# Where the split tensors begin in SBUF: stationary and moving operands at multiples of 64 bytes modulo 256

## What is computed

```python
for l in range(DEPTH):                                   # DEPTH = 2
    x = x + 0.5 * swiglu(rms_norm(x, norm_ffn1[l]), ffn1_in[l], ffn1_out[l])
    h = rms_norm(x, norm_mix[l])
    proj = h @ w_in[l]                                   # 1024 x 5504
    ...                                                  # rwkv7 mixer, differential attention
    y = jnp.einsum('bsgc,gcd->bsgd', branches, w_branch[l])
    merged = jnp.sum(gates * y, axis=2)
    x = x + merged @ w_out[l]
    x = x + 0.5 * swiglu(rms_norm(x, norm_ffn2[l]), ffn2_in[l], ffn2_out[l])

def swiglu(h, w_in, w_out):
    gate, up = jnp.split(h @ w_in, 2, axis=-1)           # 1024 x 5632
    return (jax.nn.silu(gate) * up) @ w_out              # 2816 x 1024
```

## Time and profile before

| | |
|---|---|
| time, median of 3 runs | 3126.2 us (3125.26 to 3131.27) |
| span of the profiled execution | 3137.0 us |
| PE busy | 2741.8 us (87%) |
| PE weight loads busy | 1826.8 us (58%) |
| DVE busy | 2121.8 us (68%) |
| ACT busy | 1310.7 us (42%) |
| DMA | 864.66 MB, mean 276 GB/s |

### The profile page before, as it was taken

How to read it: one execution, slowest core, us unless ns; L and a number is a source line. 1 busy time by engine, 2 the same in 40 slices (tenths; PEclk the granted TensorE clock), 3 DMA queues, 4 the chain that set the end, 5 groups by cost and what they waited for, 6 DMA issues and landing times. The chain is left out here.

```text
span 3137.0 us, 45631 instructions
## 1 busy us (share of the span) xinstructions
PE 2741.8 (87%) x17006; PEld 1826.8 (58%) x17006; DVE 2121.8 (68%) x3931; ACT 1310.7 (42%) x2970; POOL 587.5 (19%) x516
## 2 busy tenths in 40 slices
PE   7999977899899998799989999877777899778776
PEld 6877776688687767687878655322322654223232
DVE  6655776686576477567655677778774677777764
ACT  4433443444443344245434244444443344444443
POOL 0000000000000000000000154444443244444442
PEclk9999999999999999889999999999999999999999
DMA  8745301586685530237761699999999699999997
GB/s 303 275 165 180 104 4 43 198 299 237 227 293 188 187 117 4 96 138 253 266 240 62 230 416 427 427 427 427 427 427 396 257 425 426 427 427 427 427 427 305
DMA packets 256749, 864.66 MB, mean 276 GB/s; under 512 B 15504, under 2 KB 139280, under 8 KB 183952
## 3 DMA queue, kind: packets, MB, share of 16 engines
q0 software_dynamic: 73728, 536.90, 40.7%
q1 hardware_dynamic: 182800, 324.85, 29.5%
HBM read 853.04 MB, written 8.65 MB: 275 GB/s over the span
## 5 line engine op out<-in xcount | busy, mean ns | idle before, releaser
L3515 POOL DMA_INDIRECT raw_weights<-peer_rows,expert_ids x208 | 236.4, 1137 | 2111.3 <-DVE expert_ids L149 1848.4
L472 PE MATMUL banks<-weight_parts_hi,normedT_hi 128*128 128x512 f32 (+2 forms) x1152 | 460.3, 400 | 41.4 <-DVE weight_parts_lo L1312 12.0
L3625 PE MATMUL banks<-raw_weights,diagonals 128*128 128x512 f32 x832 | 396.3, 617 | 88.2 <-ACT diagonals L182 88.1
L474 PE MATMUL banks<-weight_parts_hi,normedT_lo 128*128 128x512 f32 (+2 forms) x1152 | 449.6, 390 | 0.0
L473 PE MATMUL banks<-weight_parts_lo,normedT_hi 128*128 128x512 f32 (+2 forms) x1152 | 449.1, 390 | 0.0
L3625 PE MATMUL banks<-query_weights,diagonals 128*128 128x512 f32 x704 | 335.7, 615 | 70.6 <-ACT diagonals L182 70.4
L158 DVE CUSTOM_DVE_ANT_0 modulation<-raw_weights,normed 128x1024 f32<-128x1024 f32 x208 | 254.9, 1226 | 128.4 <-DMA raw_weights<-peer_rows,expert_ids 117.0
L3625 PEld LDWEIGHTS banks<-raw_weights,diagonals 128*128 128x128 f32 x832 | 153.0, 194 | 322.6 <-ACT diagonals L182 178.8
L182 ACT ACTIVATE gelu<-dots 128x1 f32<-128x1 f32 x512 | 102.2, 200 | 500.2 <-DVE dots L158 499.4
L3625 PE MATMUL banks<-modulation,diagonals 128*128 128x512 f32 x512 | 250.8, 626 | 65.2 <-ACT diagonals L182 64.8
L158 DVE CUSTOM_DVE_ANT_0 modulation<-query_weights,normed 128x1024 f32<-128x1024 f32 x176 | 215.9, 1227 | 115.3 <-DMA query_weights<-peer_rows,expert_ids 105.7
(11 more groups left out here) (410 smaller groups left out, 4515.0 us busy)
## 6 DMA issues: line engine op xcount, KB each, us to landing
raw_weights<-ffn_in SPq DMA_DIRECT2D x88, 1024.0 KB, 7.5
side_weights<-mod_tiles SPq DMA_DIRECT2D x48, 1024.0 KB, 5.2
raw_weights<-ffn_out SPq DMA_DIRECT2D x44, 1024.0 KB, 6.6
raw_weights<-w_in SPq DMA_DIRECT2D x28, 1024.0 KB, 5.0
query_weights<-peer_w_q SPq DMA_DIRECT2D x16, 1024.0 KB, 10.7
raw_weights<-w_in SPq DMA_DIRECT2D x10, 1536.0 KB, 6.6
raw_weights<-w_branch SPq DMA_DIRECT2D x8, 1024.0 KB, 7.1
raw_weights<-w_out SPq DMA_DIRECT2D x8, 1024.0 KB, 5.4
```

What stands on the lines that cost most here:

```text
L472: nc.tensor.matmul(out, lhs.hi, rhs.hi, start=start, stop=False)
L474: return nc.tensor.matmul(out, lhs.lo, rhs.hi, start=False, stop=stop)
L3515: nc.gpsimd.indirect_dma_start(out=ring.rows(g), out_offset=None, in_=table, in_offset=bass.IndirectOffsetOnAxis(ap=ids[:, n, t:t + 1], ax ...
L3625: last = nc.tensor.matmul(k.bank(2 * j + half), diag[:, g % DIAGS, :], ring.rows(g)[:, D + half * BANK:D + (half + 1) * BANK], start=t == ...
```

## The change

`split_sb` gets a parameter `at` with a place for `_hi` and one for `_lo`; ahead of each of the two tensors a filler of up to 224 bytes a partition is allocated (`begin`), so that the tensor starts at that many bytes modulo 256. Without the parameter the place is 0. Moving tensors (`weight_parts`) are put at 128 everywhere outside of the feed-forwards; each of the four feed-forward pairs gets a pair of places of its own, from two tables. No instruction is added, removed or moved: the programs of both kernels are the same word for word on all five engines, apart from line numbers and addresses. 27 fillers are added; tensors that are allocated behind them in the same stage move by the same bytes. In the second model nothing moves but the weight tile of its first projection.

```diff
+LINE = 256
+FIRST_LINES = [((0, 0), (64, 64)), ((64, 0), (0, 128))]
+SECOND_LINES = [((0, 0), (128, 128)), ((0, 128), (0, 0))]
...
+    def begin(self, ctx, at=0):
+
+        base = -(-self.nc.sbuf_base // 32) * 32
+        gap = (at - base) % LINE
+        if gap:
+            self.sb("to_the_next_line", [P, gap // 4], ctx=ctx)
...
-def split_sb(k, name, shape, ctx):
-    return Split(k.sb(name + "_hi", shape, F32R, ctx), k.sb(name + "_lo", shape, F32R, ctx))
+def split_sb(k, name, shape, ctx, at=(0, 0)):
+    both = []
+    for half, line in zip(("_hi", "_lo"), at):
+        k.begin(ctx, line)
+        both.append(k.sb(name + half, shape, F32R, ctx))
+    return Split(*both)
...
-        parts = split_sb(k, "weight_parts", [P, 2, size], c)
+        parts = split_sb(k, "weight_parts", [P, 2, size], c, (128, 128))
...
-def swiglu(k, gain, w_in, w_out, ahead, side_part, extra=()):
+def swiglu(k, gain, w_in, w_out, ahead, side_part, extra=(), still=(0, 0), moving=(128, 128)):
...
-        hT = split_sb(k, "normedT", [P, KC, SEQ], c)
+        hT = split_sb(k, "normedT", [P, KC, SEQ], c, still)
         rs = k.sb("root", [P, NT], ctx=c)
-        actT = split_sb(k, "hiddenT", [P, NF, SEQ], c)
+        actT = split_sb(k, "hiddenT", [P, NF, SEQ], c, still)
         gated = k.sb("hidden", [P, 4, 256], ctx=c)
-        parts = split_sb(k, "weight_parts", [P, 2, size], c)
+        parts = split_sb(k, "weight_parts", [P, 2, size], c, moving)
...
     swiglu(k, gain(0), w_first, sum_weights(mat("ffn1_out"), NF, after(w_first)), w_proj, side(range(0, 12)),
-           [(k.C[:, BANK:], k.table_dram[:, BANK:])] if l == 0 else ())
+           [(k.C[:, BANK:], k.table_dram[:, BANK:])] if l == 0 else (), *FIRST_LINES[l])
...
-    swiglu(k, gain(2), w_up, sum_weights(mat("ffn2_out"), NF, after(w_up)), ahead, side(range(12, 24)))
+    swiglu(k, gain(2), w_up, sum_weights(mat("ffn2_out"), NF, after(w_up)), ahead, side(range(12, 24)), (), *SECOND_LINES[l])
```

More of the change, by code:

```diff
@@ L990, in linear_sum_stage @@
     with ExitStack() as c, nc.Block() as block:
-        parts = split_sb(k, "weight_parts", [P, 2, step * D], c)
+        parts = split_sb(k, "weight_parts", [P, 2, step * D], c, (128, 128))
         @block.tensor
@@ L2415, in way_out @@
         mT = split_sb(k, "mergedT", [P, KC, SEQ], c)
-        parts = split_sb(k, "weight_parts", [P, 3, quarter], c)
+        parts = split_sb(k, "weight_parts", [P, 3, quarter], c, (128, 128))
         jobs = [([src[:, j, i * P:(i + 1) * P] for i in range(4)], oT[n][:, :, j * P:(j + 1) * P])
```

## The result

The changed kernel takes 3132.0 us (median of 20 runs, 3129.2 to 3138.6) against 3126.8 of the kernel before (20 runs, the three of the table above among them). The ratio is 1.0017, 95% interval 1.0011 to 1.0023: 5.2 us slower, between 3.4 and 7.2. The prediction was 3106.2, so the forecast fell; the time is close to that of rival B at one step (3130).

The account below looks back on a forecast made before the run. PE's matmuls were taken to bound the split-operand stages, DMA the part from 1800 us. 3120 uncovered matmuls at 6.4 ns gave 20.0 us, distance and fillers nothing: 3126.2 - 20.0 = 3106.2 us, range 3096 to 3131.

Parts of the forecast that it names:

- rival B: Matmuls whose operands move apart pay more: one step gives 3130 us, two give 3155; chance 0.13, 0.08 at one step.
- the two prices: In PE's stages the same 128x512 matmul costs one of two prices, start to start, 6.5 ns apart.
- Term (1): Dear matmuls, one operand at an odd multiple of 32: starts at multiples of 64 save 6.4 ns each, 20.0 us uncovered.
- Term (2): In most stages operand starts now lie 64, 128 or 192 bytes apart; taken to cost zero.
- D: Among the four feed-forwards, some get the step and others pay one; 3110 to 3122 us, chance 0.06.
- A: On about 3800 uncovered matmuls, keeping operands apart lowers the cheap price too; 3082 us, 3061 at the bound; chance 0.11.
- C: Dear group's price belongs to 24 matmuls in a row into one bank, so places change nothing; 3126 us, chance 0.08.
- The size of the gain: Over the dear stages, 3120 uncovered matmuls at 6.4 ns each were to bring 20.0 us.
- fixed step for all widths: Matmuls at 384 and 448 columns were to drop by the same 6.4 ns as at 512.
- the proportional 4.8: At 384 columns, the lower bound in ns of the drop per matmul if the penalty grows with width.
- The tight tiles: Six of forty loop tiles with long DVE side work: period 11.32 us, 0.03 under the chain, costing 0.2 us at most.

Follow-up runs that it names:

- all pairs equal: Changed kernel with stationary and moving operands of every stage starting at the same byte modulo 256; 3121.3 us against 3126.2 of the kernel before, ratio 0.998.
- the mixed one: Kernel with all pairs equal, except the 384-column stage back at 32 bytes apart and 448 columns at 64; 3121.5 us against 3129.8 of the kernel before, ratio 0.9968.
- half the side work: Kernel with all pairs equal, second half of each step of the side sums left out; first products 133.0, 132.8, 132.9, 132.9 us, 1.8 us less in all.
- the kernel with the first products alone: Equal starts only in the feed-forwards' first products, other stages at the distances of the kernel before; 3122.2 us against its 3130.5, ratio 0.998.

## Why the prediction was wrong

**What bounds the kernel, and the two prices.** Right. The stages are PE's, a price from start to start is the view that tells them apart, the expert layers only moved, and ACT and DVE took no notice of the starts.

**Term (1), "exactly one of the two at an odd multiple of 32": the step that failed.** In the kernel before, "both at 64" and "both alike" are the same rows: every cheap pair was equal, every dear pair was both unequal and half odd. The rows could not tell the two causes apart, and I took the one that makes the change a gain. The runs separate them: both at 32, 226.7 ns, cheap; 0 and 128, 233.3, dear. The matmuls of that sum gained 3.0 + 0.7 us instead of 20.0.

**Term (2), distance at zero: the same mistake from the other side.** That 32 and 96 cost the same speaks against a price that grows with distance. It says nothing against a price for being apart at all, which is what was at stake. The bound above that I gave, one step of 6.4 ns on the matmuls that were cheap, is what F2's and F3's second products pay (+6.5); the second products and the branch and output products together lost 7.2 us.

**Rival B** had the mechanism and nearly the time (3130 at one step), at a chance of 0.08. Its "against" was weak: that what penalises "would have to be alike at 32, 96, 64 and 128". It is not alike (64 pays a third), so **D**, "pairs differ", is true as well: F1 to F4 read 229, 233, 233 and 231. **A** falls: no distance tried at 512 columns was cheaper than equality. **C** falls by normedT's runs of 24, which read 226.7 where the starts are equal.

**The size of the gain, had (1) been right.** The kernel with all pairs equal is what (1) promised, and it brought 6.3 us, not 20; the mixed one brought 10. By the steps of the sum: the first products went down by 5.3 ns, not 6.4, since the first rounds after each turn stay dear (1920 x 5.3 = 10.2 us). The 384 and 448 columns went down by 2.6 each, so the "fixed step for all widths" was wrong, and the proportional 4.8, given as the least, too (384 x 2.6 + 144 x 2.6 = 1.4). `w_in` at 512 columns has a covered first tile that I had not taken off (576 x 5.9 = 3.4). Together 15.0. The tight tiles took some 1.5, not 0.2: the chain's end was right (11.34 to 11.35 us behind the predecessor's start, 11.42 in the second tile of each pair), but I compared it with the period itself, as if PE went on in the same moment. The tile needs the turn and its first step behind the split, so a tight tile has 11.58 and loses 0.2, and the one with the gap gains nothing (of the 1.8 us that half the side work gives back, its 0.3 were lost before the change too). That leaves 13.5.

The rest lies in good part in the two 384-column stages. They took 49.5 us each, where the sum has them 0.5 under the 48.5 of before: 2.9 us. With them the sum is 10.6, just above the 6.3 (2.2 to 10.3) of that kernel; the same working for the mixed one gives 9.9, beside a measured 10.0 (6.3 to 13.8), and for the changed kernel +3.5 + 2.7 = +6.2, beside +5.2 (3.4 to 7.2). This takes the one profiled execution of each kernel for all its runs, which isn't shown. A part may be the clock: over its runs the granted clock averages 0.9746 against 0.9756 of the kernel before, 3.1 us more of (1 - clock) x time; over 143 runs one such us goes with 0.37 us of time within a kernel, so 1 us. Whether the clock falls more *because* matmuls are denser isn't shown, and the last few us of that kernel stay open.

**The range** ended at B's 3130 and a little, 1 us short of the time. B's own terms gave +4.3 (24.3 - 20.0) on 3126.2, so 3130.5; the measured prices give +3.5 and the runs +5.2. Of the 1.5 us up to 3132.0, 0.6 is the kernel before itself, which stands at 3126.8 over 20 runs. What the chances lacked was weight on B, not width.

## What to carry to other kernels

When two causes fit the same rows, look for the row that would separate them, and if there is none, price the change under both before choosing: here the cheap group was "equal" and "even" at once. Put a stationary and a moving operand at equal starts modulo 256 bytes as the first thing to try at 512 columns (226.8 against up to 237 ns), and measure, since at 448 columns 64 bytes apart was better. A gain of a few ns a matmul comes home only where the engine that feeds the next tile has slack: here VectorE had 0.3 us or less in six tiles of forty.

## What the runs showed of the hardware

- The price of one and the same matmul with its weight load lies between 226.8 and 236.7 ns at 512 columns, with nothing changed but the starts of its two operands in their partitions. A distance of 256 costs what 0 costs, and the sign counts (4 costs 236.7 and 252 costs 227.0 in the second product; 64 costs 228.9 and 192 costs 233.3). The Trainium skill, "SBUF — State Buffer", section "Specifications (TRN2)", has lines of 16 bytes with a penalty for each crossing to a new one. Starts at multiples of 16 all cross as many lines, so by that rule they would cost the same; these runs have 226.8, 231.7, 228.9 and 233.3 ns there.
- At the 1.2 GHz level the same operands cost 427 ns a matmul, which is 512 columns at that clock and no more. The kernel with all pairs equal, PE's timeline behind the wait in `w_in`, 11 steps in 4.70 us:

```profile
314.38 0.63 PE L487 MATMUL banks<-weight_parts_lo,normedT_hi 128*128 128x512 f32 x1
...
319.08 0.63 PE L486 MATMUL banks<-weight_parts_hi,normedT_hi 128*128 128x512 f32 x1
```

  So the excess over the columns (226.8 against 512 / 2.4 = 213.3) is there at the upper level alone. A stretch of 3.4 us at the lower one holds 8 matmuls where 15 would go: 1.6 us lost if nothing covers it, as much as an edit here brings to a whole stage. In the cases shown it comes right behind a wait of PE or a few us into a stage, and its place moves from kernel to kernel, which is why single profiles had to be compared stage by stage.
- After PE has turned a hidden tile, with equal starts, the next five to ten matmuls cost 232 ns before the price settles at 226.7. At narrower widths it can settle at either of two prices with the same starts. In the kernel with the first products alone, the 384-column stage (32 bytes apart) has 22 steps in 3.88 us, 176.4 ns, ahead of its stretch at the lower clock, and 24 in 4.16 us, 173.3, behind it; the mixed kernel, with the same starts, has 176.7 behind that stretch too.

```profile
225.37 0.34 PE L487 MATMUL banks<-weight_parts_lo,normedT_hi 128*128 128x384 f32 x1
...
229.25 0.34 PE L488 MATMUL banks<-weight_parts_hi,normedT_lo 128*128 128x384 f32 x1
...
244.81 0.34 PE L487 MATMUL banks<-weight_parts_lo,normedT_hi 128*128 128x384 f32 x1
...
248.97 0.34 PE L487 MATMUL banks<-weight_parts_lo,normedT_hi 128*128 128x384 f32 x1
```

  So at 384 and 448 columns a price read in one kernel need not come back in the next. At 512 columns no stage with equal starts settled anywhere but at 226.7. A pair's price is thus not a property of the pair alone but of how the stream before it ran; that fits the failure of both pair rules, and is as far as these runs reach.
